# Expert weights in 2 MB transfers of 16 KB pieces, biases kept on chip, and another order of the gate chunks

## Reference

```python
h = rms_norm(x, attn_norm_g)
proj = h @ w_in                       # 29 chunks of 256 columns: q, k, v of three branches and their gates
y_a = neighbourhood_attention(qa, ka, va, na_rpb) @ w_branch_a
y_b = dilated_mixture(qb, kb, vb, t5_bias)        @ w_branch_b
y_c = memory_attention(qc, mk, mv)                @ w_branch_c
x = x + (g0 * y_a + g1 * y_b + g2 * y_c) @ w_out
h = rms_norm(x, ffn_norm_g)
for each expert e, over its rows xb of h:
    gu = xb @ w_gate_up[e] + b_gate_up[e]         # 1024 x 2048 weights: 8 MB
    g, u = min(gu[:, :1024], 7), clip(gu[:, 1024:], -7, 7)
    a = (u + 1) * (g * sigmoid(1.702 * g))
    y += weight * (a @ w_down[e] + b_down[e])     # 1024 x 1024 weights: 4 MB
out = rms_norm(x + y, final_norm_g)
```

## Time and profile before

| | |
|---|---|
| median of three runs | 1306.06 us (1302.8 to 1310.84) |
| profiled execution, own time | 1304.99 us |
| its span, first to last instruction | 1303.2 us |
| TensorE matmul busy | 1231.7 us, 95% of the span |
| VectorE, ScalarE, GpSimd busy | 274.2, 274.2, 220.7 us |
| packets of SP's DMA queue | 116812, 455.42 MB, 88.2% of 16 engines |
| mean granted TensorE clock | 0.96 |

### The profile page before, as it was taken

How to read it: one execution, slowest core, us unless ns; L and a number is a source line. 1 busy time by engine, 2 the same in 40 slices (tenths; PEclk the granted TensorE clock), 3 DMA queues, 4 the chain that set the end, 5 groups by cost and what they waited for, 6 DMA issues and landing times.

```text
span 1303.2 us, 16823 instructions
## 1 busy us (share of the span) xinstructions
PE 1231.7 (95%) x6611; PEld 626.5 (48%) x6611; DVE 274.2 (21%) x495; ACT 274.2 (21%) x555; POOL 220.7 (17%) x95
## 2 busy tenths in 40 slices
PE   6999997999899999999999999999989999999996
PEld 6998986898443333333333333333333333333332
DVE  3156265232311111111111111111202111111112
ACT  6455355344101110110001101100101010001002
POOL 6776665684100000000000000000000000000000
PEclk9999998999899999999998999999989899999999
DMA  9655443675799999999999999999999999999992
GB/s 322 212 174 166 154 142 107 210 265 206 324 360 416 416 416 417 417 417 418 417 418 418 417 417 417 417 417 417 418 418 418 418 418 418 417 418 416 417 416 98
DMA packets 117032, 456.29 MB, mean 350 GB/s; under 512 B 7318, under 2 KB 47950, under 8 KB 84189
## 3 DMA queue, kind: packets, MB, share of 16 engines
q1 hardware_dynamic: 116812, 455.42, 88.2%
q0 software_dynamic: 176, 0.26, 0.1%
HBM read 454.58 MB, written 1.07 MB: 350 GB/s over the span
## 4 chain that ended last, share of the span: by engine, by line
PE 52%; SPq 26%; DMA 12%; DVE 3%; issue 3%; ACT 2%; POOL 2%; DVEq 0%; POOLq 0%; ACTq 0%
PE ps L477 50%; SPq L342 22%; DMA arena<-in_expert_b_gate_up 11%; SPq L388 3%; POOL w_parts L464 2%; ACT arena L870 1%; DVE arena L1101 1%; PE ps L522 1%; DMA arena<-in_w_mem_kv 1%; DVE row_max L1111 1%; DVE neg_max L1118 0%; PE ps L729 0%; DVE arena L1108 0%; SPq L432 0%; PE ps L739 0%
## 5 line engine op out<-in xcount | busy, mean ns | idle before, releaser
L477 PE MATMUL ps<-arena,gathered_T 128*64 128x512 f32 x2048 | 452.0, 594 | 0.0
L477 PE MATMUL ps<-arena 128*64 128x512 f32 (+5 forms) x1482 | 353.4, 615 | 1.9 <-ACT arena L968 0.9
L477 PEld LDWEIGHTS ps<-arena,gathered_T 128*64 128x64 f32 x2048 | 143.8, 137 | 280.1 <-issue 279.3
L477 PEld LDWEIGHTS ps<-arena 128*64 128x64 f32 (+3 forms) x1482 | 118.6, 159 | 230.8 <-issue 225.9
L464 POOL TENSOR_TENSOR w_parts<-arena,w_parts 128x1024 fp32r<-128x1024 f32 x84 | 211.5, 2543 | 94.1 <-ACT w_parts L850 92.2
L1216 DVE TENSOR_SCALAR arena<-ps 128x512 f32<-128x512 f32 x32 | 22.1, 691 | 754.2 <-PE ps L477 754.2
L850 ACT CAST w_parts<-arena 128x1024 fp32r<-128x1024 f32 x82 | 81.8, 1045 | 119.6 <-PE ps L477 117.8
L477 PE MATMUL ps<-w_parts,h_T_parts 128*128 128x256 f32 x816 | 102.0, 283 | 0.2 <-POOL w_parts L464 0.2
L477 PEld LDWEIGHTS ps<-w_parts,h_T_parts 128*128 128x128 f32 x816 | 99.1, 188 | 4.2 <-issue 3.0
L477 PE MATMUL ps<-arena,ones 1*64 1x512 f32 (+1 forms) x262 | 70.0, 649 | 32.6 <-DMA arena<-in_expert_b_gate_up 32.6
L968 ACT COPY arena<-ps 128x512 f32<-128x512 f32 x32 | 18.8, 586 | 329.8 <-PE ps L477 329.8
(11 more groups left out here) (156 smaller groups left out, 576.9 us busy)
## 6 DMA issues: line engine op xcount, KB each, us to landing
arena<-in_expert_w_gate_up SPq DMA_DIRECT2D x256, 1024.0 KB, 20.1
arena<-in_expert_w_down SPq DMA_DIRECT2D x128, 1024.0 KB, 24.8
arena<-in_w_in SPq DMA_DIRECT2D x29, 1024.0 KB, 5.3
arena<-in_w_mem_kv SPq DMA_DIRECT2D x4, 1024.0 KB, 12.6
arena<-in_w_out SPq DMA_DIRECT2D x4, 1024.0 KB, 9.5
arena<-t_scratch SPq DMA_DIRECT2D x6, 384.0 KB, 3.9
arena<-in_w_branch_a SPq DMA_DIRECT2D x2, 1024.0 KB, 5.0
arena<-in_w_branch_c SPq DMA_DIRECT2D x2, 1024.0 KB, 4.9
```

The source lines that it names most:

```text
L477: return nc.tensor.matmul(out, lhsT, rhs, start=start, stop=stop, **kw)
```

## The change

Four edits, and what they bring with them:

1. An expert's weights come in six transfers of 2 MB, four of gate and up and two of down, each with one piece of 16 KB for each partition. A partition now gets two neighbouring rows of gate and up (four of down), so that rows are paired: the gather takes every second column of the normalised tokens, the activation is turned with every fourth column, and the gain of the gathered rows comes from a fourth, re-ordered copy of `ffn_norm_g`. TensorE waits for a landing once for two chunks, and SP for the second of two chunks to be used.
2. `("in", 26)` moves from behind `("branch_a", 1)` to ahead of it; step 12 then stands behind `("in", 26)` and step 13 behind `("branch_a", 1)`.
3. The gate and up biases of all experts are loaded once, in four transfers of 64 KB, and kept in two parts (`bias_parts`: ScalarE's rounded copy, and on 64 partitions VectorE's remainder). `pick` holds for the next expert a 0/1 matrix, copied by VectorE once for each expert; two matmuls of 128x128 by 512 columns in fp32r write the bias. For expert 0 they run behind its fourth gate-up chunk. The 32 bias loads, their semaphores and TensorE's waits on them go.
4. TensorE's code for the experts is straight for all 32.

```diff
-         + [("branch_a", 0), ("in", 25), ("branch_a", 1), ("in", 26), ("in", 27), ...
+         + [("branch_a", 0), ("in", 25), ("in", 26), ("branch_a", 1), ("in", 27), ...
-EARLY_AFTER = {36: (0, 1), 37: (2, 3), 38: (4, 5)}
+EARLY_AFTER = {36: 0, 37: 2, 38: 4}
-    w_gu = t["expert_w_gate_up"].rearrange("l e (k p) c -> (l e) p k c", p=P)
-    w_dn = t["expert_w_down"].rearrange("l e (k p) c -> (l e) p k c", p=P)
+    w_gu = t["expert_w_gate_up"].rearrange("l e (k p a) c -> (l e) p k (a c)", p=P, a=2)
+    w_dn = t["expert_w_down"].rearrange("l e (k p a) c -> (l e) p k (a c)", p=P, a=4)
...
+                sp.dma_start(ring[:, r:r + 2, :].rearrange("p r c -> p (r c)"), src).then_inc(landed[r], 16)
...
+            def load_bias():
+                for part in range(2):
+                    for h in range(2):
+                        row = EXPERTS * (2 * part + h)
+                        sp.dma_start(bias_raw[row:row + EXPERTS], b_gu[0].rearrange("e (b h c) -> h e b c", b=2, h=2)[h]
+                                     ).then_inc(bias_in, 16)
...
-                        sp.wait_ge(chunk_used, NF + c - RING + 1)
+                        sp.wait_ge(chunk_used, NF + c - RING + 2)
...
-            for j in range(EARLY, EXPERT_CHUNKS):
-                if j == EXPERT_CHUNKS - 1:
+            for j in range(EARLY, EXPERT_CHUNKS, 2):
+                if j == EXPERT_CHUNKS - 2:
...
+                if j == 8:
+                    sp.wait_ge(chunk_used, OUT0)
+                    load_bias()
...
-                        last = mm(ps[:, bank, k * P:k * P + width], xn[:, tt, (4 * half + k) * P:(4 * half + k + 1) * P],
+                        last = mm(ps[:, bank, k * P:k * P + width], xn_pairs[:, tt, 2 * half + k // 2, :, k % 2],
...
-            def bias_rows(n, bias_slot, bias_fill):
-                pe.wait_ge(brow_in[bias_slot], bias_fill)
-                pe.wait_ge(gu_drained, n + 1)
+            def bias_rows(pick_slot, first=True):
                 for b in range(2):
-                    for h in range(2):
-                        mm(ps[64 * h:64 * h + 64, b, :], ones[64 * bias_slot:64 * bias_slot + 1, 0:BLK],
-                           brow[64 * bias_slot:64 * bias_slot + 1, b * D + 512 * h:b * D + 512 * (h + 1)], True, False)
+                    mm(ps[:, b, :], pick[:, pick_slot, :], bias_parts[:, b, :], first, False, skip_group_check=True)
...
-                    last = nc.tensor.transpose(ps[:, 2, f * P:(f + 1) * P], sig[:, f * P:(f + 1) * P], ident[:])
+                    last = nc.tensor.transpose(ps[:, 2, f * P:(f + 1) * P], sig.rearrange("p (q f) -> p f q", f=4)[:, f, :], ident[:])
...
-            bias_rows(0, 0, 16)
-            four_experts(0)
-            with pe.Fori(1, EXPERTS // 4 - 1) as it:
-                four_experts(it)
-            four_experts(EXPERTS // 4 - 1, True)
+            for it in range(EXPERTS // 4):
+                four_experts(it, it == EXPERTS // 4 - 1)
...
+            act.wait_ge(bias_in, 64)
+            nc.scalar.copy(bias_parts[:], bias_raw[:]).then_inc(bias_high, 1)
             act.wait_ge(top_ready, 1)
...
+            dve.wait_ge(bias_high, 1)
+            lows = slice(2 * EXPERTS, 4 * EXPERTS)
+            vec.tensor_copy(pick[:, 0, :].rearrange("p (h s) -> p h s", h=2), bcast(pick_raw[:, :, 0], 2, BLK)).then_inc(pick_ready, 1)
+            vec.tensor_tensor(bias_parts[lows], bias_raw[lows], bias_parts[lows].bitcast(F32), ALU.subtract).then_inc(bias_ready, 1)
...
+            def pick_rows(pick_slot, e):
+                vec.tensor_copy(pick[:, pick_slot, :].rearrange("p (h s) -> p h s", h=2),
+                                bcast(pick_raw[:, :, bass.ds(e, 1)].rearrange("p h o -> p (h o)"), 2, BLK)).then_inc(pick_ready, 1)
```

More of the change, by code:

```diff
@@ L220, in moe @@
             return area(at, *dims)
-        brow = moe(2 * D)
+        pick = split_at("pick", place[0], 2, 2 * BLK)
+        moe(2 * 2 * BLK)
         b_dn = moe(D)[0:EXPERTS, :]
         final_g = moe(D)
+        sig, y_sb = moe(512), moe(512)
+        place[0] = MOE0 + 2 * KC * S
         iota = moe(D)
@@ L258, in build @@
         branch_evac = sem("branch_evac")
-        brow_in = [sem(f"brow_in{i}") for i in range(2)]
+        bias_in, bias_high, bias_ready, pick_ready = sem("bias_in"), sem("bias_high"), sem("bias_ready"), sem("pick_ready")
         out_saved = sem("out_saved")
@@ L404, in wait_for @@
                     r = ring_slot(c)
-                    if j == 0 and n >= 2:
-                        sp.wait_ge(chunk_used, NF + EXPERT_CHUNKS * (n - 2) + 1)
                     if c >= RING:
-                        sp.wait_ge(chunk_used, NF + c - RING + 1)
+                        sp.wait_ge(chunk_used, NF + c - RING + 2)
                     elif r < FRONT_RING:
-                        sp.wait_ge(chunk_used, max(i for i in range(NF) if i % FRONT_RING == r) + 1)
+                        sp.wait_ge(chunk_used, max(i for i in range(NF) if i % FRONT_RING in (r, r + 1)) + 1)
                     elif r < SCORE_SLOT:
@@ L456, in _ @@
             pool.dma_start(stack4[:], t["stack4"]).then_inc(consts_in, 16)
+            pool.dma_start(pick_raw[:], t["pick"]).then_inc(consts_in, 16)
             pool.dma_start(rw[:], t["router_w"].rearrange("l (k p) e -> (l p) k e", p=P)).then_inc(consts_in, 16)
@@ L657, in _ @@
             turn_x1(3)
[L658 removed]
+            xn_pairs = xn[:].rearrange("p t (k q a) -> p t k q a", k=4, a=2)
+            pe.wait_ge(consts_in, 96)
             for c in range(4):
@@ L1214, in expert @@
                 last.then_inc(PW_ready, 1)
+                if pick_next is not None:
+                    pick_rows(pick_next, n + 1)
                 dve.wait_ge(chunk_used, NF + EXPERT_CHUNKS * n + KC)
@@ L1235, in _ @@
                         last.then_inc(P_ready, 1)
-                    expert(n, keys, iota[:, 0:BLK], bass.ds(n, 1))
+                    expert(n, keys, iota[:, 0:BLK], bass.ds(n, 1), (q + 1) % 2)
             dve.wait_ge(routed, 1)
@@ L1285, in constants @@
     na_mask = np.tile(np.where(ok, 0.0, NEG).astype(np.float32), (P // GRID_W, 1))[::-1].copy()
-    return {"bucket_onehot": onehot, "group_of_head": group, "na_mask": na_mask, "ident": np.eye(P, dtype=np.float32),
+    pick = np.zeros((2, 2, EXPERTS, 2, EXPERTS + 1), np.float32)
+    for h in range(2):
+        pick[:, h, np.arange(EXPERTS), h, np.arange(EXPERTS)] = 1.0
+    return {"pick": pick.reshape(P, 2, EXPERTS + 1), "bucket_onehot": onehot, "group_of_head": group, "na_mask": na_mask, "ident": np.eye(P, dtype=np.float32),
             "stack4": np.tile(np.eye(EXPERTS, dtype=np.float32), (4, 1)),
@@ L1300 @@
     arrays.update(constants())
+    paired = np.asarray(inputs["ffn_norm_g"]).reshape(KC // 2, P, 2).transpose(0, 2, 1).reshape(KC, P)
     arrays["g_rows"] = np.concatenate([np.asarray(inputs[n]).reshape(KC, P)
-                                       for n in ("mem_norm_g", "attn_norm_g", "ffn_norm_g")], 0)
+                                       for n in ("mem_norm_g", "attn_norm_g", "ffn_norm_g")] + [paired], 0)
     rpb = np.asarray(inputs["na_rpb"])[0]
```

71 lines of the change are left out of this document (37 added, 34 removed).

## The result

The changed kernel takes 1273.03 us (median of four runs, 1272.51 to 1273.4), the kernel before 1304.81 beside it. The ratio is 0.9751, 95% interval 0.9726 to 0.9776: 2.5% faster. Taken again on another chip it is 1272.18, ratio 0.9762 (0.9749 to 0.9776). The forecast was 1265.0, within 1255 to 1290. The profiled execution has a span of 1271.6 us against 1303.2, which is 31.6 less where 40.0 were forecast.

The account below looks back on a forecast made before the run. The weight stream was taken as the bound. Expert 2's start at 361.5 + 2.1 + 879.3 + 1 gave a stream end of 1243.9, then the last chain a span of 1263.2; forecast time 1265.0 us, range 1255 to 1290.

Parts of the forecast that it names:

- Pieces: Expert weight stream: 16 KB pieces save fixed time of 9 ns a piece, -0.86 us an expert, -25.8 over 30 experts.
- Rival A: Expert weight stream: piece size gives nothing, only biases and front do, 1291 us; chance within a shared 0.22 for 1276 to 1293.
- The 358 GB/s of the Trainium skill: HBM to SBUF: a rule that about 358 GB/s binds a core, 35.1 us an expert in pieces of any size.
- Bias loads: Weight stream: each 8 KB bias occupies one engine 0.31 us and slows every landing; removing 30 gives -9.3 us.
- Instruction fetches: Straight TensorE code adds 23 packets of 16 KB, 0.6 us each on an engine; spread +0.9, on one engine +14; taken +1.
- no second straggler: End of the stream before: existing instruction packets left no second late engine, the ground for taking only +1 us.
- The gate chunk: Between the halves of `branch_a`: moved chunk fills TensorE's 7.63 us of idle, -7.0, with 1.6 given back to the clock: -5.4.
- Start of the experts: Expert 0's gate-up product starts 5.4 + 1.9 us earlier, at 334.0; expert 2's first transfer at 361.5.
- rival B: TensorE becomes the bound: stepped operands add x us an expert, passing the forecast at x = 2.2; slower beyond 3.8, chance 0.06.
- the 2 us held for them in the last chain: Last chain after the stream: 2 us added for wider steps of gather and transposes, span 1261.2 to 1263.2.
- Rival C: Gaps between landings cost TensorE its clock: 3 us an expert would show, end chain up to 3, 1267; small form within 0.62.
- End of the stream: Stream ends at 1243.9 with all engines within 2 us; last gate-up pair lands at 1234.1, last down product ends at 1249.8.

Follow-up runs that it names:

- the two kernels with the old pieces: Changed kernel, 2 MB transfers kept but in pieces of 8 KB (gate, up) and 4 KB (down): 1294.47 us; with TensorE's code for experts 4 to 27 looped, 1289.01.
- the row that nobody waits for: Changed kernel, TensorE's code looped, SP's straight, plus two unread 4 KB bias pieces for each of experts 1 to 31: 1277.29 us; without the pieces 1268.77.
- The old pieces with the loop: Changed kernel with 2 MB transfers in 8 KB and 4 KB pieces, and TensorE's code for experts 4 to 27 in a loop: 1289.01 us, ratio 0.9898.
- the order alone: Kernel before with only the gate chunk moved between the halves of the neighbourhood product: 1300.46 us, ratio 0.9964.
- the loop version: Changed kernel with TensorE's code for experts 4 to 27 in a loop again: 1269.65 us, ratio 0.9725; on another chip 1268.35, ratio 0.9732.

## Why the prediction was right, and what it mis-sized

The direction, the mechanism and the bound were right: the weight stream sets the pace before and after. The span came out at 1271.6 for 1263.2. The 8.4 us are these.

**Pieces.** Right, with a term a little too large. Forecast 429 GB/s and 25.8 us, measured 428 and about 22: 30 x (30.14 - 29.40) = 22.2, and 20.7 to 22 by the runs. The forecast subtracted two figures that were not got alike: 30.17 us for an expert of before is from the rate of the stream, 29.31 for one of after from the times of single pieces. By single pieces on both sides it is 30.04 - 29.31 = 0.73 an expert, 21.9 in all, which is what came. Rival A (1291) is what the two kernels with the old pieces gave, 1289 and 1294, and it was not the case. The 358 GB/s of the Trainium skill, which the prediction set aside, stays set aside by every window above. Another page of the Trainium skill says why: by "Perfetto Trace Analysis", section Roofline, 358 is a core's share when both cores of a pair are active, and about 435 GB/s is what the 16 engines of a single active core can carry. An estimate from that page is that 428 leaves under 2% for any further piece size. No run here tried a larger piece.

**Bias loads.** Right within what the runs can tell: forecast 9.3 us, and the row that nobody waits for gives 8.5 by itself. The old pieces with the loop stand 8.6 us below the order alone by the ratios (0.9898 and 0.9964, 1303 us) and 11.5 by the medians, from two chips; they differ in the biases, and in 2 MB for 1 MB. Their profiles say it more closely: expert 2 starts at 361.08 and 361.30 us, and the last weights have landed at 1269.8 and 1278.0. The four new transfers cost nothing that shows, and the new work on ScalarE and VectorE is hidden where it was expected. From the timeline of the kernel after:

```profile
320.34 1.03 ACT L956 CAST bias_parts<-bias_raw 128x1024 fp32r<-128x1024 f32 x1
...
323.65 0.53 ACT L959 ACTIVATE arena<-arena 128x32 f32<-128x32 f32 x2 [0.98 <-DVE arena L1170]
...
329.13 1.22 DVE L1207 TENSOR_TENSOR bias_parts<-bias_raw,bias_parts 64x1024 fp32r<-64x1024 f32 x1
...
335.90 0.74 DVE L1194 TENSOR_SCALAR arena<-arena 128x64 f32<-128x64 f32 x4 [0.71 <-PE ps L483]
```

ScalarE's idle 1.92 us is 0.98 now and VectorE's 2.15 is 0.71: both were eaten into and neither was used up.

**Instruction fetches.** The term that failed: +1, measured +3.8. Two steps of it were wrong. A packet was taken at 0.6 us, the time of a weight piece of that size, though the row that was quoted says otherwise: 5 packets with 0.3% of 16 engines over 130 us are 1.0 to 1.5 us each, and by the landing times one sets its engine back by about 1.6. And "spread over the engines" was taken as all sixteen, when the packets fell on eight of them and a landing waits for the worst. That no second straggler stood at the end of before was true, and no evidence: beside an engine 10 us behind, three us can't be seen.

**The gate chunk.** At its place it is exact. TensorE of the kernel after, for the earlier trace rows:

```profile
203.23 7.84 PE L483 MATMUL ps<-w_parts,h_T_parts 128*128 128x256 f32 x64
214.56 5.61 PE L483 MATMUL ps<-w_parts,h_T_parts 128*128 128x256 f32 x32 [3.49 <-POOL w_parts L470]
...
221.98 5.78 PE L483 MATMUL ps<-w_parts,attention_parts 128*128 128x512 f32 x24
```

The wait ends at 214.56 (forecast 214.4). The plain sum had the second half end some 7 us early and 1.6 given back; the steps that both orders share end 5.5 us earlier than before. But only 3.8 of these reach the router. Both kernels have three short waits for `merged_T_parts` near 290 us, and a low clock behind them. The windows, after first, then before at the same work:

```profile
290.00:294.00 4.00, 2.83 (x10) 2.20 (x11) 1.14 (x2) 1.90 (x3) 2.05 (x1) 0.58 0.81 225
294.00:298.00 4.00, 4.00 (x23) 4.00 (x22) 0.00 (x0) 0.17 (x1) 0.00 (x0) 0.56 0.98 416
298.00:302.00 4.00, 4.00 (x35) 4.00 (x35) 0.69 (x1) 2.00 (x2) 1.18 (x1) 1.00 0.06 20
```

```profile
295.00:299.00 4.00, 3.08 (x13) 2.17 (x11) 1.62 (x3) 1.31 (x2) 2.55 (x1) 0.65 0.61 193
299.00:303.00 4.00, 3.97 (x33) 3.97 (x34) 0.00 (x0) 0.76 (x2) 0.00 (x0) 1.00 1.01 422
```

Before, the full clock is back when the long row of products behind the waits starts (299), now only some 5 us after its start (298 for 292.7): 1.6 us lost, the same in the kernel with the order alone. Why the chip gives the clock back later there is open.

**Start of the experts.** Forecast 334.0, and it was late by 3.0:

```profile
336.96 7.09 PE L483 MATMUL ps<-arena,gathered_T 128*64 128x512 f32 x32 [1.23 <-ACT gathered_T L966]
343.98 0.74 PE L483 MATMUL ps<-bias_parts,pick 128*128 128x512 f32 x2
```

1.6 is the clock, and 1.2 is a wait that the sum had not looked for. The four products for expert 0's bias (1.93 us) had stood where TensorE would else wait for ScalarE to move the gathered rows; taken away, they uncover 1.23 us of it. The forecast counted the whole 1.93 as gained. SP's first transfer of expert 2 then goes out at 364.14, for 361.5.

**TensorE, and rivals B and C.** An early expert of the kernel after, for the earlier trace rows:

```profile
427.57 0.44 PE L738 MATMUL ps<-ident,arena 128*128 128x128 f32 x2
...
436.88 2.15 PE L483 MATMUL ps<-arena,x_normed 128*128 128x128 f32 x16
438.87 0.64 PE L748 MATMUL ps<-ident,arena 128*128 128x128 f32 x4
439.26 0.70 PE L483 MATMUL ps<-bias_parts,pick 128*128 128x512 f32 x2
440.31 7.09 PE L483 MATMUL ps<-arena 128*64 128x512 f32 x32 [0.34 <-DVE arena L1248]
...
454.19 0.44 PE L738 MATMUL ps<-ident,arena 128*128 128x128 f32 x2
```

454.19 - 427.57 = 26.62 us, forecast 26.5. The stepped operands cost 0.10 and 0.04: x of rival B is 0.14, where 2.2 was needed to matter, and the 2 us held for them in the last chain were not used. The old pieces with the loop, without the steps, have 2.05 and 0.60 again. The stepped operands are those that TensorE loads as weights (PEld). Those of the transposes, in the kernel after and then in the old pieces with the loop (mean ns behind the busy time):

```profile
L748 PEld LDWEIGHTS ps<-ident,arena 128*128 128x128 f32 x120 | 16.8, 205 | 0.0
```

```profile
L750 PEld LDWEIGHTS ps<-ident,arena 128*128 128x128 f32 x120 | 14.1, 141 | 0.0
```

With the step of four a load takes 205 ns instead of 141, with the step of two in the gather 196 instead of 191. But a load overlaps with the product before it, and the matmul records grow by only 7 to 9 ns each. The rule of the Trainium skill on lines of SBUF, named in the prediction, has the step of two free and the step of four not: the loads agree in kind. Of the 0.6 us that the prediction's estimate from that rule put on the transposes, TensorE's time shows 0.04. Rival C falls as well, and in an unexpected way: the more frequent gaps leave the clock at 1.00, the rare long ones of before had it at 0.94.

**End of the stream.** The last gate-up pair lands at about 1244.1, forecast 1234.1. Of the 10 us, 2.6 are the later start, 2.8 the fetches beyond the 1 us, and 2.7 the rate (29.40 for 29.31 in 30 experts). The other 2 fit to what even the loop version shows: its engines end 3.2 us apart, and the sum had them end together. From there the chain went as written: 1260.20 - 1244.18 = 16.0 us to the end of the last down product for 15.7, and then 11.4 us to the end of the span in both kernels. 10.1 for the last landing, 0.3 for the chain and 2 not used: 10.1 + 0.3 - 2 = 8.4.

The terms as measured, against before: pieces -20.7 (by the runs of one chip) to -22.2 (by the rates), bias loads -8.5 (the row that nobody waits for), front and start -3.4 (367.51 to 364.14), straight code +3.8. That is -28.8 to -30.3 for the 31.6 of the spans, and 1 to 3 us are not assigned.

## What to carry to other kernels

Where the share of the DMA engines is 1, ask what a piece costs one engine (here 9 to 10 ns beyond its bytes) and count the pieces: size of transfer (1 or 2 MB) did not matter, size of piece did. A stream over 16 engines is as fast as the one that is furthest behind, so a small load on a single partition costs its full time there, even when nobody waits for it; look at the last windows of the stream for a share of one sixteenth, and once that is cured for engines dropping out one by one. And when products are taken out of TensorE, look at what they were covering: the wait that comes to light is subtracted from the gain.

## What the runs showed of the hardware that was not expected

- An instruction packet of 16 KB sets one DMA engine back by 1.2 to 2.1 us in a full stream, where a weight piece of that size takes 0.6. The packets fell on eight of the sixteen engines, and twenty more of them put 3.6 us on the last landing of 400 MB of weights.
- One engine's lag does not grow without end: with a bias brought twice it stopped at 11 to 12 us by the landing times, where the ring of 16 slots let the other engines run dry, and from there the rate of all fell from 417 to 404 to 414 GB/s.
- Waits of up to 1.3 us, 53 of them from 340 us on, leave the clock at 1.00 in the window of 1000 to 1200 us, while 17 waits of up to 3.3 us had it at 0.94 there.
- A row written as sixteen neighbouring parts went out as one piece.
- A 128x128 weight load for TensorE from every fourth float32 column took 205 ns where neighbouring columns took 141, from every second 196 for 191; of this 7 to 9 ns a product showed in TensorE's time.
